# Moving two adaLN steps behind the norm's transposes at the change of layers, in a two-layer hybrid transformer step

## The chip, the core and the metric

One Trainium2 chip, one of its cores. TensorE (PE) multiplies, VectorE (DVE) and ScalarE (ACT) do elementwise work, GpSimd (POOL) some adds and small DMAs, and SyncE's queue (SP) issues the large weight loads. The metric is the device time of one execution in microseconds (us), as the median of several runs.

## The reference, cut to what matters

Two token groups of 128 tokens (a context group, g = 0, and a latent group, g = 1) go through the same two layers. All data are float32.

```python
def layer(x, cond, l, p, ctx):
    mod = jnp.einsum('...d,de->...e', jax.nn.silu(cond), p['w_ada'][l]) + p['b_ada'][l]
    sh1, sc1, g1, sh2, sc2, g2 = jnp.split(mod.reshape(-1, 1, 6 * D_MODEL), 6, axis=-1)
    hn = rmsnorm(x, p['norm_mix'][l]) * (1.0 + sc1) + sh1
    mix, ctx_tensors = token_mixers(hn, l, p, ctx)      # attention, retention, HGRN2; w_in, w_out
    x = x + g1 * mix
    hn = rmsnorm(x, p['norm_ffn'][l]) * (1.0 + sc2) + sh2
    x = x + g2 * moe(hn, l, p)                          # 16 experts, top 2 of the best group
    return x, ctx_tensors
```

D_MODEL is 1024; `w_ada` (1024 x 6144 a layer) makes the modulation, which people call adaLN; `w_in` is 1024 x 3840, and an expert has three matrices of 1024 x 512.

## The kernel before

Each engine has its own program, and semaphores order them. A `Ledger` counts what every semaphore has been raised to, so a wait names a label, such as `("xn1", 0, 1)`, and gets the right count. Both groups live in SBUF as rows, `x[:, g, :]`, and as features, `hnT`, eight chunks of 128 features by 256 tokens.

**Loads.** SP issues the weight loads of 1 MB each into `ring`, eight slots in turn, and into a few other tiles (`eP`, `wT` and the `home_` tiles), in one order fixed by hand. Before each load it waits until PE has released the slot. PE releases a slot with a later matmul: the slot's name is put on the list `owed`, and the next matmul that is given to `pay` raises the semaphore. An instruction of this kernel carries one increment, so a matmul that signals something else doesn't pay.

**adaLN steps.** The modulation of two of the six vectors, for both groups, is one accumulation over eight steps. `ada_step(l, what, k)` waits for one slot of `w_ada` and runs four matmuls of 512 columns, each with 32 columns of `silT` as its stationary side, into the four 32-partition strips of bank 1. The steps are spread over the kernel to keep PE busy while other engines work. Five of them, `IN_CHANGE`, which are the steps k = 0 to 4 of `(1, "g")`, stand at the change from layer 0 to layer 1. SP issues their loads behind the two loads of the first block of `w_in` ("f", into `eP` and `wT`).

**End of a layer.** The experts run in eight turns (a loop whose body is one round of all eight). In the last turn, and after it, `gates_to_all(g)` copies the gate row g2 of a group to all 128 partitions: for each half of 512 columns one matmul with 32 rows, from rows 64 to 95 of `modG` into bank 0 and from rows 96 to 127 into bank 1; ACT takes both halves into `gbuf2[g]`, which are the tiles `sq` and `t1`. Then four matmuls add the last turn's rows to banks 4 to 7 (group 0 halves 0 and 1, group 1 halves 0 and 1). DVE multiplies each bank by its gate half. The first half of a group goes to `first_product[g]` and POOL adds it to `x` (line 2019); the second goes to `nsq` and DVE adds it (line 1675).

**Start of layer 1.** ACT sums the squares of each group's row and makes 1/rms into `stat` (lines 1725, 1697, 1692). `normed("xn1", g)` on DVE scales the row in two halves into `xs` (line 1159). PE's `normalized_group` transposes the halves (four 128 x 128 blocks each), and `shifted` on DVE, or on ACT for the last half of group 1, applies scale and shift on the way into `hnT` (lines 1186 and 1762). The projection block "f" follows: `by_head_and_group` takes group 0 first, then transposes group 1 and takes that; then come `by_head("f", 1)`, "q", "a" and the first matmuls of HGRN2, `diagonal`, which wait for DVE's `gates` and `queries`.

Line 479 of the profile is `mm`, line 514 the transposes of `bank_of_transposes`, line 546 those of `normalized_group`, line 1673 DVE's product with the gate.

Of the kernel before, what the change touches and what calls it, by code (L numbers as in the profile page):

```python
# [15 lines left out]
P = 128  # L16
D = 1024
KC = D // P
L = 2
NG = 2  # L20
# [25 lines left out]
AT_CHANGE = 5  # L46
# [161 lines left out]
def build(nc, io, known, final=False):  # L208
# [3 lines left out]
    led = Ledger(known)  # L212
# [3 lines left out]
    with ExitStack() as ctx:  # L216
        sems = {}

        def S(name):
            if name not in sems:  # L220
                sems[name] = ctx.enter_context(nc.semaphore(name))
            return sems[name]
# [4 lines left out]
        ps = ctx.enter_context(nc.psum_tensor("ps", [P, 8, BLK], f32))  # L227
# [7 lines left out]
        modX, modG = sb("modX", BLK), sb("modG", BLK)  # L235
        modTs = sb("modT", L, 4, KC, NG)
        C = {}
# [123 lines left out]
        IN_CHANGE = [(1, "g", k) for k in range(AT_CHANGE)]  # L361
# [111 lines left out]
        def _(pe):  # L473
# [4 lines left out]
            def mm(*a, **k):  # L478
                ins = nc.tensor.matmul(*a, **k)  # L479
                return ins  # L480

            def pay(ins):

                if owed:
                    s = owed.pop(0)
                    ins.then_inc(S(f"{s}_spent" if s in KEPT else f"slot{s}_used"), 1)
                return ins
# [49 lines left out]
            def normalized_group(stage, factors, g, ahead=None, first=None):  # L537

                xv = xs[:, g].rearrange("p (k q) -> p k q", k=KC)
                for h in range(2):  # L540
                    b = claim_for_norm() if h or first is None else first
                    if not h and ahead is not None:
                        ahead(b)
                    pe.wait_ge(c.of(factors, g, h), c.at(factors, g, h))
                    for k in range(KH):
                        last = nc.tensor.transpose(ps[:, b, k * P:(k + 1) * P], xv[:, KH * h + k, :], C["ident"][:])  # L546
                        if k < KH - 1:
                            pay(last)
                    last.then_inc(c.fills(b, stage + "T", g, h), 1)
# [32 lines left out]
            for l in range(L):  # L582
# [3 lines left out]
                def modulation_by_feature(l, norm, b=0):  # L586
# [6 lines left out]
                            pay(last)  # L593
                    last.then_inc(c.fills(b, "modT", l, norm), 1)

                def at_change(b):

                    for step in IN_CHANGE:
                        ada_step(*step)

                if l == 0:
                    b = claim_for_norm()
                    for step in EARLY[0:5]:
                        ada_step(*step)
                        stream_zeros(b, 3)
                    pe.wait_ge(c.of("begin_dma"), c.at("begin_dma"))
                    normalized_group("hn1", "xn1", 0, first=b)
                    normalized_group("hn1", "xn1", 1)
                    for step in EARLY[5:]:
                        ada_step(*step)  # L610
                    modulation_by_feature(0, 0)
                else:
                    normalized_group("hn1", "xn1", 0, at_change)

                def wait_for_input(g, half):
                    label = ("hn1S", g, half) if l else (f"hn1S{g}", half)
# [25 lines left out]
                def by_head_and_group(name, p, ss, b):  # L642

                    for g in range(NG):
                        if l and g:
                            normalized_group("hn1", "xn1", 1)
                        for hl in range(2):
                            h = 2 * p + hl
                            for k in range(KC):
                                if not hl and not k % KH:  # L650
                                    wait_for_input(g, k // KH)
                                for d in range(2):
                                    col = 64 * h + 256 * d
                                    last = mm(ps[64 * d:64 * d + 64, b, 256 * hl + P * g:256 * hl + P * (g + 1)], by_k(ss[k // KH], 512)[:, k % KH, col:col + 64], hnT[:, k, tok(g)], start=(k == 0), stop=(k == KC - 1), skip_group_check=True)
                                    if not (g and hl and k == KC - 1 and d):
                                        pay(last)
                    last.then_inc(c.fills(b, "projP", name, p), 1)
# [329 lines left out]
                with pe.Fori(c.cum[l], until) as r:  # L987
# [42 lines left out]
                    def gates_to_all(g):  # L1030

                        for h in range(2):
                            pe.wait_ge(S(f"bank{h}_free"), c.claim(h))
                        for h in range(2):
                            strip = slice(32 * (2 + h), 32 * (2 + h) + 32)
                            row = 32 * (2 + h) + g
                            mm(ps[:, h, :], C["ident"][strip, row:row + 1].broadcast_to([32, P]), modG[strip, :], start=True, stop=True).then_inc(c.fills(h, "gate2P", g, h), 1)

                    pe.wait_ge(c.of("bias"), c.at("bias"))
                    gather()  # L1040
# [63 lines left out]
                    for g in range(NG):  # L1104
                        for h in range(2):
                            pe.wait_ge(c.of("ys", h), c.at("ys", h))
                            last = mm(ps[:, 4 + 2 * g + h, :], seatT[t % 3][:, g, :], ys[:, h, :], start=False, stop=True, skip_group_check=True)
                            if g or h:
                                last.then_inc(c.makes(f"round_sums{2 * g + h}", 0), 1)
                            else:  # L1110
                                pay(last)
                c.cum[l + 1] = count_of_rounds(pe, l + 1)
                led.where = f"A{l}"
                for b in range(4, 8):
# [5 lines left out]
        def _(dve):  # L1120
# [5 lines left out]
            def st(ins, *label):  # L1126

                ins.then_inc(c.makes(*(label or (step[0],))), 1)
                dve.wait_ge(S(c.last[0]), c.last_value())
# [21 lines left out]
            for l in range(L):  # L1151
# [3 lines left out]
                def normed(stage, g):  # L1155
                    dve.wait_ge(c.of(stage + "r", g), c.at(stage + "r", g))
                    for h in range(2):
                        half = slice(h * BLK, (h + 1) * BLK)
                        st(ts(xs[:, g, half], x[:, g, half], stat[:, g, 2:3], None, ALU.mult), stage, g, h)
# [12 lines left out]
                    st(stt(out=modTs[:, l, 2 * norm + 1], in0=modTs[:, l, 2 * norm + 1], scalar=1.0, in1=nrmTs[:, l, norm].rearrange("p (k o) -> p k o", o=1).broadcast_to([P, KC, NG]), op0=ALU.add, op1=ALU.mult), "modS", l, norm)  # L1172


                normed("xn1", 0)
                if not l:
                    normed("xn1", 1)
                def shifted(stage, a, halves):

# [485 lines left out]

                step[0] = "dve_step"
                led.where = f"A{l}"
                dve.wait_ge(S("gate2"), c.value("gate2", f"A{l}", 0))
                for g in range(NG):
                    for h, to in enumerate((first_product[g], nsq[:])):  # L1670
                        sums = f"round_sums{max(2 * g + h, 1)}"
                        dve.wait_ge(S(sums), c.value(sums, f"A{l}", 0))
                        tt(to, ps[:, 4 + 2 * g + h], gbuf2[g][:, h * BLK:(h + 1) * BLK], ALU.mult).then_inc(c.freed(("y", 2 * g + h), "x2p", g, h), 1)
                        dve.wait_ge(S(c.last[0]), c.last_value())
                    st(tt(x[:, g, BLK:D], x[:, g, BLK:D], nsq[:], ALU.add), "x2", g)


        @block.scalar
        def _(acte):
# [35 lines left out]
            for l in range(L):  # L1715
# [212 lines left out]
                with acte.Fori(c.cum[l], c.cum[l + 1]) as r:  # L1928
                    c.t = r
                    led.where = f"T{l}"  # L1930
                    step[0] = "act_turn"

                    def gathered(t):

                        led.turn = t
                        for half in range(2):
                            evac(("xT", half), None, "xTs", half, fn=lambda src: nc.scalar.copy(xT[:, KH * half:KH * (half + 1), :], src.rearrange("p (k s) -> p k s", k=KH)))  # L1937

                    gathered(0)
                    for t in range(TURNS):  # L1940
                        led.turn = t
                        acte.wait_ge(c.of("gu", 0), c.at("gu", 0))
                        st(ex_(ge, ps[:, 2], -1.0), "gexp")
                        evac(("actT",), None, "actTs", fn=lambda src: nc.scalar.copy(actT, src.rearrange("p (k s) -> p k s", k=KE)))  # L1944
                        if t + 1 < TURNS:
                            gathered(t + 1)
                            led.turn = t
                        else:
                            for h in range(2):
                                evac(("gate2P", 0, h), gbuf2[0][:, h * BLK:(h + 1) * BLK])  # L1950
                        evac(("yP", 0), ys[:, 0], "ys", 0)
                    for h in range(2):
                        evac(("gate2P", 1, h), gbuf2[1][:, h * BLK:(h + 1) * BLK])
                    acte.sem_inc(c.makes("gate2"), 1)
                step[0] = "act_step"
                led.where = f"A{l}"

# [195 lines left out]
```

## Time and profile before

| | us |
|---|---|
| median of 3 runs | 928.63 |
| lowest and highest of them | 927.77, 929.88 |
| the profiled execution's own time | 925.69 |
| its span, first to last instruction | 923.9 |

The profiled execution was somewhat faster than all three timed runs. PE is busy 875.4 us of the span (95%), its weight loads (PEld) 446.1 us, DVE 457.1 us (49%), ACT 165.3 us, POOL 79.5 us; the DMA engines moved 307.36 MB at a mean of 333 GB/s, and 420 GB/s where they are full. The first projection of layer 1 begins at about 484 us of the span. A matmul of 128 x 512 float32 is two records in the trace, and records of PE overlap, so the distance between starts tells more than a duration.

### The profile page before, as it was taken

How to read it: one execution, taken by the hardware profiler on the slowest of the kernel's cores; microseconds unless marked ns; L12 is line 12 of the kernel's file. 1: busy time of each engine (PE TensorE's matmuls, PEld its weight loads, DVE VectorE, ACT ScalarE, POOL GpSimd, SP SyncE). 2: the span in 40 equal slices, each digit the busy share in tenths (PEclk: the TensorE clock that was granted, in tenths of full speed). 3: DMA queues.
4: the chain of work that ended last, by engine and by line, in shares of the span. 5: the costliest groups of instructions: out<-in, count | busy, mean ns of one | idle time of the engine just before them, and what ended most of it. 6: DMA issues, size and time to landing. Idle time of an engine off the chain costs nothing.

```text
span 923.9 us, 13303 instructions
## 1 busy us (share of the span) xinstructions
PE 875.4 (95%) x4752; PEld 446.1 (48%) x4758; DVE 457.1 (49%) x839; ACT 165.3 (18%) x428; POOL 79.5 (9%) x110
## 2 busy tenths in 40 slices
PE   5899999999999999999989999999998999999997
PEld 1655565568733333333327455756874333333332
DVE  2485887653563332332236887876357322333222
ACT  2212015221211111110021301432220111111011
POOL 1112230000010000000011223000001000000001
PEclk9999999999999999999999999999999999999999
DMA  8997665868789999999996565474568999999992
GB/s 362 415 404 290 228 253 204 319 270 342 298 338 423 420 419 421 420 420 421 420 414 226 218 221 200 183 299 180 234 267 316 423 419 420 420 420 422 419 420 98
DMA packets 50316, 307.36 MB, mean 333 GB/s; under 512 B 8682, under 2 KB 8698, under 8 KB 16848
## 3 DMA queue, kind: packets, MB, share of 16 engines
q1 hardware_dynamic: 42368, 291.52, 78.1%
q0 software_dynamic: 4848, 12.40, 3.6%
q10 hardware_dynamic: 3040, 2.62, 0.8%
q8 instruction: 39, 0.64, 0.3%
q14 instruction: 21, 0.17, 0.0%
HBM read 305.46 MB, written 4.73 MB: 336 GB/s over the span
## 4 chain that ended last, share of the span: by engine, by line
PE 81%; DMA 7%; DVE 7%; issue 2%; ACT 1%; SPq 1%; DVEq 0%; ACTq 0%
PE ps L479 77%; PE ps L514 4%; DMA wT<-in_w_in 3%; DMA ring<-in_w_experts 3%; DMA ring<-in_w_ada 2%; DVE fa L1261 1%; DVE rt L1132 1%; PE ps L546 1%; SPq L392 0%; ACT eP L1692 0%; DVE xy L1267 0%; DVE proj L1595 0%; DVE hnT L1186 0%; DVE home_es L1278 0%; DVE proj L1305 0%
## 5 line engine op out<-in xcount | busy, mean ns | idle before, releaser
L479 PE MATMUL ps<-ring,proj 128*64 128x512 f32 x1024 | 283.2, 596 | 2.7 <-ACT proj L1944 1.7
L479 PE MATMUL ps<-ring,hnT 128*128 128x512 f32 (+1 forms) x576 | 204.4, 506 | 3.2 <-DVE hnT L1516 1.0
L479 PEld LDWEIGHTS ps<-ring,proj 128*64 128x64 f32 x1024 | 87.8, 137 | 138.7 <-issue 138.7
L479 PEld LDWEIGHTS ps<-ring,hnT 128*128 128x128 f32 x576 | 106.7, 191 | 77.6 <-issue 69.7
L1663 DVE COPY proj<-ps 128x512 f32<-128x512 f32 x16 | 11.1, 691 | 129.4 <-PE ps L479 129.4
L479 PE MATMUL ps<-home_ra,proj 128*64 128x512 f32 x128 | 57.6, 593 | 4.8 <-issue 4.8
L479 PE MATMUL ps<-ring,silT 128*32 128x512 f32 x384 | 47.6, 616 | 14.0 <-DMA ring<-in_w_ada 7.1
L479 PE MATMUL ps<-home_kd,proj 128*64 128x512 f32 x128 | 57.8, 594 | 0.0
L479 PE MATMUL ps<-home_qc,proj 128*64 128x512 f32 x128 | 57.6, 593 | 0.0
L1649 DVE RECIPROCAL proj<-proj 128x512 f32<-128x512 f32 x16 | 53.6, 3353 | 0.6
L1648 DVE TENSOR_SCALAR proj<-proj 128x512 f32<-128x512 f32 x16 | 6.8, 427 | 80.8 <-ACT proj L1692 80.8
L479 PE MATMUL ps<-hnT,ring 128*128 128x256 f32 x192 | 43.6, 382 | 0.0
L479 PE MATMUL ps<-proj,modX 128*128 128x512 f32 x80 | 38.7, 606 | 0.0
L479 PEld LDWEIGHTS ps<-hnT,ring 128*128 128x128 f32 x192 | 35.7, 190 | 5.9 <-issue 1.2
L479 PEld LDWEIGHTS ps<-home_ra,proj 128*64 128x64 f32 x128 | 17.1, 137 | 41.9 <-issue 41.8
L479 PEld LDWEIGHTS ps<-xy 64*128 64x128 f32 (+1 forms) x480 | 29.9, 188 | 12.0 <-issue 11.1
L1937 ACT COPY proj<-ps 128x512 f32<-128x512 f32 x32 | 18.7, 585 | 91.6 <-PE ps L514 75.0
L1944 ACT COPY proj<-ps 128x512 f32<-128x512 f32 x16 | 9.4, 585 | 143.6 <-PE ps L514 143.6
L479 PEld LDWEIGHTS ps<-home_qc,proj 128*64 128x64 f32 x128 | 17.4, 137 | 35.6 <-issue 35.3
L1692 ACT ACTIVATE proj<-ps 128x512 f32<-128x512 f32 x16 | 9.6, 597 | 128.2 <-PE ps L479 128.2
L479 PE MATMUL ps<-xy 64*128 64x64 f32 (+1 forms) x480 | 32.0, 275 | 0.1
L1692 ACT ACTIVATE eP<-ps,rt 128x128 f32<-128x128 f32 (+1 forms) x64 | 26.2, 417 | 23.2 <-DVE rt L1426 22.6
(271 smaller groups left out, 1054.0 us busy)
## 6 DMA issues: line engine op xcount, KB each, us to landing
ring<-in_w_experts SPq DMA_DIRECT2D x128, 1024.0 KB, 15.4
ring<-in_w_ada SPq DMA_DIRECT2D x48, 1024.0 KB, 9.8
ring<-in_w_in SPq DMA_DIRECT2D x24, 1024.0 KB, 8.5
home_qc<-in_w_experts SPq DMA_DIRECT2D x16, 1024.0 KB, 13.9
home_ra<-in_w_experts SPq DMA_DIRECT2D x16, 1024.0 KB, 18.0
home_kd<-in_w_experts SPq DMA_DIRECT2D x16, 1024.0 KB, 19.4
ring<-in_w_out SPq DMA_DIRECT2D x8, 1024.0 KB, 11.0
eP<-in_w_experts SPq DMA_DIRECT2D x4, 1024.0 KB, 10.4
```

What stands on the lines that cost most here:

```text
L479: ins = nc.tensor.matmul(*a, **k)
L514: last = nc.tensor.transpose(ps[:, b, i * P:(i + 1) * P], src, C["ident"][:])
L546: last = nc.tensor.transpose(ps[:, b, k * P:(k + 1) * P], xv[:, KH * h + k, :], C["ident"][:])
L1132: return v.tensor_reduce(out=out, in_=in_, axis=AX, op=op)
L1261: st(v.reciprocal(R, R))
L1648: st(ts(ge, ge, 1.0, None, ALU.add))
L1649: st(v.reciprocal(ge, ge))
L1663: v.tensor_copy(ys[:, 1], ps[:, 3]).then_inc(c.freed(("yP", 1), "ys", 1), 1)
L1692: return act_(out, in_, AF.Exp, scale=scale, **k)
L1937: evac(("xT", half), None, "xTs", half, fn=lambda src: nc.scalar.copy(xT[:, KH * half:KH * (half + 1), :], src.rearrange("p (k s) -> p k s ...
L1944: evac(("actT",), None, "actTs", fn=lambda src: nc.scalar.copy(actT, src.rearrange("p (k s) -> p k s", k=KE)))
```

## The change

1. `at_change` runs three of the five steps of `IN_CHANGE` ahead of group 0's transposes (`AT_CHANGE - NG` = 3). The fourth follows those transposes, the fifth the transposes of group 1.
2. `normed("xn1", 0)` of layer 1 moves on DVE: it stands between the two products of group 1 and the last addition, that of `x`'s second half of group 1.
3. Each of the banks 4 to 7 signals by its own matmul (`round_sums0` is new; the first matmul paid a slot before). DVE waits for its own bank, and for the gate of its own group (`gate2_0`, `gate2_1` for `gate2`).
4. `gates_to_all` splits each of its two matmuls of 512 columns into two of 256. The first part of each pays, since the first sum no longer does. All four calls of a kernel run (two groups, two layers) are split.

```diff
                 def at_change(b):
-                    for step in IN_CHANGE:
+                    for step in itertools.islice(in_change, AT_CHANGE - NG):
                         ada_step(*step)
...
                     normalized_group("hn1", "xn1", 0, at_change)
+                    ada_step(*next(in_change))
...
                         if l and g:
                             normalized_group("hn1", "xn1", 1)
+                            ada_step(*next(in_change))
...
-                            mm(ps[:, h, :], C["ident"][strip, row:row + 1].broadcast_to([32, P]), modG[strip, :], start=True, stop=True).then_inc(c.fills(h, "gate2P", g, h), 1)
+                            for part_ in range(2):
+                                sl = slice(256 * part_, 256 * (part_ + 1))
+                                last = mm(ps[:, h, sl], C["ident"][strip, row:row + 1].broadcast_to([32, P]), modG[strip, sl], start=True, stop=True)
+                                if not part_:
+                                    pay(last)
+                            last.then_inc(c.fills(h, "gate2P", g, h), 1)
...
-                            if g or h:
-                                last.then_inc(c.makes(f"round_sums{2 * g + h}", 0), 1)
-                            else:
-                                pay(last)
+                            last.then_inc(c.makes(f"round_sums{2 * g + h}", 0), 1)
...
-                normed("xn1", 0)
                 if not l:
+                    normed("xn1", 0)
                     normed("xn1", 1)
...
-                dve.wait_ge(S("gate2"), c.value("gate2", f"A{l}", 0))
                 for g in range(NG):
+                    dve.wait_ge(S(f"gate2_{g}"), c.value(f"gate2_{g}", f"A{l}", 0))
                     for h, to in enumerate((first_product[g], nsq[:])):
-                        sums = f"round_sums{max(2 * g + h, 1)}"
+                        sums = f"round_sums{2 * g + h}"
                         dve.wait_ge(S(sums), c.value(sums, f"A{l}", 0))
                         tt(to, ps[:, 4 + 2 * g + h], gbuf2[g][:, h * BLK:(h + 1) * BLK], ALU.mult)...
+                    if g and l + 1 < L:
+                        c.l, led.where = l + 1, f"L{l + 1}"
+                        normed("xn1", 0)
+                        c.l, led.where = l, f"A{l}"
                     st(tt(x[:, g, BLK:D], x[:, g, BLK:D], nsq[:], ALU.add), "x2", g)
...
                         evac(("yP", 0), ys[:, 0], "ys", 0)
+                    acte.sem_inc(c.makes("gate2_0"), 1)
                     for h in range(2):
                         evac(("gate2P", 1, h), gbuf2[1][:, h * BLK:(h + 1) * BLK])
-                    acte.sem_inc(c.makes("gate2"), 1)
+                    acte.sem_inc(c.makes("gate2_1"), 1)
```

## Rows read from the trace of the kernel before

**Rows 1.** The page's chain that ended last: shares of the span by engine

```profile
PE 81%; DMA 7%; DVE 7%; issue 2%; ACT 1%; SPq 1%; DVEq 0%; ACTq 0%
```

**Rows 2.** The chain in order of time, 460 to 520: start, duration, what

```profile
464.73 16.28 DMA ring<-in_w_ada
...
518.73 1.27 PE ps L479 x9
```

**Rows 3.** Timeline of PE: start, duration, operation, records, [idle before <-releaser]

```profile
469.28 1.13 PE L479 MATMUL ps<-modG,c_begin 32*128 32x512 f32 x4
470.33 3.70 PE L479 MATMUL ps<-proj 128*128 128x512 f32 x8
473.97 3.04 PE L479 MATMUL ps<-ring,silT 128*32 128x512 f32 x24
478.50 1.06 PE L479 MATMUL ps<-ring,silT 128*32 128x512 f32 x8 [1.49 <-DMA ring<-in_w_ada]
481.05 1.07 PE L479 MATMUL ps<-ring,silT 128*32 128x512 f32 x8 [1.49 <-DMA ring<-in_w_ada]
482.05 1.09 PE L546 MATMUL ps<-c_begin,xs 128*128 128x128 f32 x8
484.17 1.09 PE L479 MATMUL ps<-hnT,eP 128*64 128x128 f32 x16 [1.02 <-DVE hnT L1186]
...
488.44 1.09 PE L546 MATMUL ps<-c_begin,xs 128*128 128x128 f32 x8
490.65 1.09 PE L479 MATMUL ps<-hnT,eP 128*64 128x128 f32 x16 [1.12 <-DVE hnT L1186]
```

**Rows 4.** Timeline of PE's weight loads, the third adaLN step among them

```profile
475.94 0.16 PEld L479 LDWEIGHTS ps<-ring,silT 128*32 128x32 f32 x8 [0.96 <-DMA ring<-in_w_ada]
```

**Rows 5.** Timeline of DVE at the change of layers

```profile
472.43 0.69 DVE L1673 TENSOR_TENSOR proj<-ps,sq 128x512 f32<-128x512 f32 x1 [2.24 <-PE ps L479]
473.15 0.69 DVE L1673 TENSOR_TENSOR nsq<-ps,sq 128x512 f32<-128x512 f32 x1
473.88 1.14 DVE L1675 TENSOR_TENSOR x<-x,nsq 128x512 f32<-128x512 f32 x1
...
476.50 1.22 DVE L1675 TENSOR_TENSOR x<-x,nsq 128x512 f32<-128x512 f32 x1
477.75 1.01 DVE L1159 TENSOR_SCALAR xs<-x,stat 128x512 f32<-128x512 f32 x2
482.74 2.87 DVE L1186 TENSOR_SCALAR hnT<-ps,modT 128x128 f32<-128x128 f32 x8 [3.98 <-PE ps L546]
```

**Rows 6.** Timeline of ACT: group 0's sum of squares and 1/rms

```profile
475.05 1.06 ACT L1725 ACTIVATE sq<-x 128x1024 f32<-128x1024 f32 x1 [3.36 <-DVE x L1675]
...
476.56 0.20 ACT L1692 ACTIVATE stat<-stat 128x1 f32<-128x1 f32 x1
```

**Rows 7.** The first gates_to_all of layer 0, its records split by narrow windows

```profile
464.64 0.70 PE L479 MATMUL ps<-modG,c_begin 32*128 32x512 f32 x2
...
465.17 0.59 PE L479 MATMUL ps<-modG,c_begin 32*128 32x512 f32 x2
```

**Rows 8.** Stretches: busy time of each engine, PE's clock, DMA share, GB/s

```profile
495.00:519.00 24.00, 23.95 (x118) 14.69 (x113) 21.50 (x28) 1.85 (x3) 4.28 (x8) 1.00 0.41 142
519.00:700.00 181.00, 174.10 (x1051) 116.55 (x1052) 124.80 (x257) 47.81 (x150) 21.93 (x32) 0.99 0.60 231
706.00:900.00 194.00, 189.70 (x858) 69.45 (x854) 62.99 (x91) 21.17 (x36) 7.09 (x7) 1.00 1.01 418
620.00:625.00 5.00, 5.00 (x21) 2.19 (x21) 4.17 (x11) 0.97 (x3) 0.00 (x0) 0.72 1.01 421
```

**Rows 9.** What SP's queue waited for, 482 to 720: us in total, times, longest

```profile
SPq L392 <- PE ps L479: 110.2, 18, 26.2
```

**Rows 10.** Timeline of DVE at the end of the kernel

```profile
915.49 0.69 DVE L1673 TENSOR_TENSOR proj<-ps,sq 128x512 f32<-128x512 f32 x1 [2.25 <-PE ps L479]
...
919.56 1.20 DVE L1675 TENSOR_TENSOR x<-x,nsq 128x512 f32<-128x512 f32 x1
```

More of the change, by code:

```diff
@@ L594, in modulation_by_feature @@
                     last.then_inc(c.fills(b, "modT", l, norm), 1)
+                in_change = iter(IN_CHANGE)
                 def at_change(b):
-                    for step in IN_CHANGE:
+                    for step in itertools.islice(in_change, AT_CHANGE - NG):
                         ada_step(*step)
```

## The prediction

> **What bounds the kernel now.** I read the chain of waits first. PE holds 81% of it and DMA 7% [rows 1], so the time moves if PE's program moves, and only there. Around the changed code the chain leaves PE: from 464.73 it follows the loads of `w_ada` for 16.28 us [rows 2]. In PE's timeline three adaLN steps begin at 473.97, the fourth at 478.50 and the fifth at 481.05, each of the last two after an idle stretch that a `w_ada` load ended, and only at 482.05 do group 0's transposes start [rows 3]. Their input was ready long before: DVE had scaled the row by 477.75 + 1.01 = 478.76 [rows 5]. So here the layer waits for the loads of two steps whose result nobody needs yet.
>
> Then I asked who is behind. From 495 to 519 PE is busy 23.95 of 24.00 us, without slack [rows 8], while the chain goes through DVE's gates and comes back to PE at 518.73 [rows 2]. Both end together, and both begin with the projections of "f". What starts these earlier moves both alike.
>
> **Part 1, the two steps behind the transposes.** Nothing is removed, two steps move. I work out when the first projection, now at 484.17 [rows 3], could start. Three things come together there.
>
> PE: the third step starts at 475.94, when its load is there [rows 4]. It takes as long as the fifth, 482.05 - 481.05 = 1.0, so PE is ready to transpose at 476.95 and done 0.87 later. The fourth step's load is there at 478.50, and the step fills PE until 479.5. The fifth, whose load is there at 481.05, runs behind group 1's transposes: there PE needs 0.87 + 1.0 = 1.9 us in a stretch that lasts 490.65 - 488.44 = 2.21 now [rows 3]. Both steps are thus nearly free, because PE sits idle for 1.02 and 1.12 us there, waiting for DVE's shift [rows 3]. Without this cover each would cost its 1.0.
>
> DVE, with parts 2 and 3 in it: the second sum of group 0 comes as before, so DVE begins its second product at 472.43 and not at 473.15; that is one product, 0.72, earlier [rows 5]. The addition behind it then ends at 474.3. ACT needs 476.56 + 0.20 - 475.05 = 1.71 for 1/rms [rows 6], so it is there at 476.03; meanwhile DVE does group 1's two products, 1.44. The scaling takes 1.01, until 477.1. Now comes the addition that it was moved ahead of. It takes 1.22 at most, as in the row; without POOL adding beside it perhaps 0.69, as the product of the same size [rows 5]. DVE is free at 477.8 to 478.35. The shift of the first half takes 484.17 - 482.74 = 1.43 [rows 3, 5], so its result is there at 479.25 to 479.8.
>
> The later of 479.5 (PE) and 479.25 to 479.8 (DVE) gives 479.5 to 479.8; I take 479.7, as the longer addition is a measured row. That is **4.5 us earlier**. What is late next is DVE: it and the fourth step end within 0.3 us of each other. Group 1's factor is late by this order, since its addition ends at 478.35 and not at 477.72, but PE wants group 1 only after 488.44 - 484.17 = 4.3 us of group 0's work; DVE finishes scaling it at about 482.2, before 484.
>
> What the move does to SP: the issue order stays. The fifth step's slot is released about 4 us later, at 486, and the load that takes it, the first of block "b", is issued later. The DMA engines are at 0.41 of their time from 495 to 519 [rows 8], and "b" is used after 519, so this costs nothing. The bounds are 0 and the 2.5 us that one load takes (481.05 - 478.50, [rows 3]).
>
> **Part 2, the scaled row ahead of the addition.** It is in the sum above. Behind the addition the scaling would end at about 478.0 rather than 477.1, and the transposes of the second half later by as much, so it is worth at most 1.0 here. It costs ACT's second factor up to 0.6, which is covered.
>
> **Part 3, each bank signals.** At the end of the kernel the same 0.72 is gained: DVE's products and additions run without a gap from 915.49 to 919.56 + 1.20 [rows 10], and the output waits for the last. Here nothing can hide it: **-0.72**. The extra waits are for things long done: DVE's first product waits for both groups' gates now, and what released it at 472.43 was PE and not ACT [rows 5]. The released slot is 1, about 2 us earlier, for a load that queues behind full DMA engines: nothing.
>
> **Part 4, the split.** The four calls lie on PE's path: the last sums come right behind them, then the three steps, and in both layers DVE starts on those sums. One call takes 470.33 - 469.28 = 1.05 [rows 3]. The trace of before has no two matmuls in a row in the same strip of rows, so I must bound the cost s of a split. The four records of a call start two by two, at 464.64 and 465.17 [rows 7]: the two strips work side by side, each pair some 0.43 us apart, as eight records take 3.64 us [rows 3]. The parts now come in the order strip 2, strip 2, strip 3, strip 3, each half as long. If the strips still run side by side, s = 0. If only neighbours of different strips pair, the middle two do and there are three stretches of 0.43 in place of two: s = 0.43. If none pairs, four: s = 0.86. I take the middle: the rows show pairing between neighbours and nothing of an overtaking. One call's cost comes twice before the change of layers (2s) and twice before the end (2s), 1.7 us in all.
>
> The Trainium skill ("TensorE: Matmul & The Clock Gate", section "Part 3: Packing small matmuls — row/col tiling") says that matmuls start and end strictly in program order, and that only weight loads are pulled ahead. This speaks against the change, and by it the sum would be the one with s = 0.43. The starts of the rows are in order and fit it, but they would fit the other too.
>
> **The sum.** At the change of layers -4.5 + 0.86 = -3.6 (the third step is then ready 0.6 later too, but DVE decides). At the end -0.72 + 0.86 = +0.1. Total **-3.5 us**. Against the profile's own execution that is 925.69 to 922.2; against the median of the runs shown, 928.63 to 925.1. I predict by the median, 3 us above the profiled execution, and this distance is itself a warning about what one run tells.
>
> **Does the gain last?** From 519 to 700 the DMA engines are at 0.60, and SP waits for PE to release slots, 110.2 us in 18 waits [rows 8, 9]. All loads move with PE. From 706 to 900 they are full at 418 GB/s [rows 8], so that stretch is a length of DMA time, but its start is set by slots that PE releases, and so it moves as well.
>
> **The rivals.**
> - *The strips keep running side by side* (s = 0). All of the -4.5 and -0.72 stays: -5.2, 923.4. For it: pairs start within a rounding in [rows 7]. Against: the second strip's matmul would have to pass a waiting one. Chance 0.28.
> - *No pairing at all* (s = 0.86): -3.0 at the change, since 2s delays only DVE's path, +1.0 at the end: -1.9, 926.7. Chance 0.15.
> - *The gain is given back to the DMA engines*: if some load between 519 and 700 isn't late because of PE but because of the queue before it, the full stretch from 706 starts when it did. Then only the end counts: +0.1, 928.8. Against it: 0.60 in [rows 8]. Chance 0.08.
> - *The split costs more than it looks, and the kernel gets slower.* If a matmul of 256 columns in a strip that is still busy takes the whole latency of one by itself, 0.59 to 0.70 [rows 7], with two records in each of four parts, one call goes from 1.05 to 8 x 0.65 = 5.2, s = 4.1. The total is -5.2 + 4s, so it is slower from s = 1.3 on, and by this price it would be 12 us slower, 940. Against it: sixteen records of 128 columns take 1.09 in the row at 490.65 [rows 3], so a short record doesn't bear a fixed latency. Chance 0.04.
> - *The clock.* Between 620 and 625 the granted clock is 0.72 [rows 8]: for a part of it PE ran at the lower of its two levels, 1.2 GHz, though busy. This costs 5 x 0.28 = 1.4 us. A shift of all that precedes may lose this stretch or add another, so 1.4 either way on any case. As the outcome that decides, 0.03.
>
> The forecast itself has 0.42.
>
> **Range and chances.** Cases of one sign hold 0.85; within them 923.4 to 926.7. With 1.4 below for the clock, and above up to the near side of the given-back gain, 922.0 to 928.2 leaves out less than 0.2. A measurement of this kernel can tell about 0.2%, 1.9 us. Faster by more: the forecast, s = 0, and half of s = 0.86, 0.77. Within 0.2%: the other half, the given-back case, some of the clock's, 0.18. Slower 0.05.
>
> **What would show it.** PE's timeline after: three steps together, group 0's transposes near 477 to 478, a fourth step behind them, and the first projection at 480 to 480.6, its wait ended by DVE's shift. If it was ended by a `w_ada` load, part 1 fails. The records of `modG`: 8 in 1.05 us (s = 0), 1.5 (the forecast) or 1.9. DVE's two scalings of group 0 ahead of the addition. `diagonal`'s first matmul at about 515 and not 518.73; if it is there but the end isn't 3.5 earlier, the later stretches took it back, and the share of DMA and the clock of these stretches tell which. DVE's last product pair should start 0.72 closer to the first sum. The prediction is wrong mainly if the split costs otherwise than I take it, for it enters four times.

## The result, and the profile after

The changed kernel takes 919.59 us as the median of 4 runs (918.78 to 921.2); the kernel before took 928.83 us in its 4 runs, 9.2 us more. The ratio of the runs is 0.9923, with a 95% interval of 0.9897 to 0.9949. Two later sets, on two chips, gave 0.9929 (0.9909 to 0.9949) and 0.9934 (0.9908 to 0.9959). Few runs make an uncertain median here, so I go by all runs that have a granted clock on record: 926.9 us is the mean of 77 runs of the kernel before, 919.8 the mean of 16 of the changed one. By these the change makes the kernel 7.1 us faster, 0.77%. The prediction had 925.1 us, 3.5 us faster, and its range ended at 922.0. Direction and places were right, the size was half of what was measured.

The profiled execution of the changed kernel has a span of 918.3 us and a time of 920.11. Its PE timeline at the change of layers answers to [rows 3]:

```profile
470.71 1.14 PE L479 MATMUL ps<-modG,c_begin 32*128 32x256 f32 x8
471.78 3.70 PE L479 MATMUL ps<-proj 128*128 128x512 f32 x8
475.41 3.00 PE L479 MATMUL ps<-ring,silT 128*32 128x512 f32 x24
478.34 1.09 PE L546 MATMUL ps<-c_begin,xs 128*128 128x128 f32 x8
479.90 1.06 PE L479 MATMUL ps<-ring,silT 128*32 128x512 f32 x8 [0.47 <-DMA ring<-in_w_ada]
480.90 1.09 PE L479 MATMUL ps<-hnT,eP 128*64 128x128 f32 x16
...
485.11 1.10 PE L546 MATMUL ps<-c_begin,xs 128*128 128x128 f32 x8
486.14 1.06 PE L479 MATMUL ps<-ring,silT 128*32 128x512 f32 x8
487.33 1.09 PE L479 MATMUL ps<-hnT,eP 128*64 128x128 f32 x16
...
515.41 2.05 PE L479 MATMUL ps<-xy 128*128 128x128 f32 x16
```

The two executions are shifted against each other by 1.4 us that arose before this place, so distances are to be compared. From the start of the last gate call to the first projection of layer 1 it was 484.17 - 469.28 = 14.89 us [rows 3]; it is 480.90 - 470.71 = 10.19. The three steps now stand together, the transposes follow at once, and the fourth step fills the wait behind them. From the first projection to `diagonal` (xy) it is 34.5 us in both: what was gained is kept. The gate call has eight records for four, and takes 471.78 - 470.71 = 1.07 us where it took 1.05.

DVE's timeline answers to [rows 5, 10]:

```profile
473.01 0.69 DVE L1679 TENSOR_TENSOR proj<-ps,sq 128x512 f32<-128x512 f32 x1 [1.40 <-PE ps L479]
473.87 0.69 DVE L1679 TENSOR_TENSOR nsq<-ps,sq 128x512 f32<-128x512 f32 x1 [0.17 <-PE ps L479]
...
477.45 1.11 DVE L1165 TENSOR_SCALAR xs<-x,stat 128x512 f32<-128x512 f32 x2 [0.40 <-ACT stat L1702]
478.60 0.69 DVE L1685 TENSOR_TENSOR x<-x,nsq 128x512 f32<-128x512 f32 x1
479.42 2.86 DVE L1192 TENSOR_SCALAR hnT<-ps,modT 128x128 f32<-128x128 f32 x8
...
909.89 0.69 DVE L1679 TENSOR_TENSOR proj<-ps,sq 128x512 f32<-128x512 f32 x1 [1.40 <-PE ps L479]
910.75 0.69 DVE L1679 TENSOR_TENSOR nsq<-ps,sq 128x512 f32<-128x512 f32 x1 [0.17 <-PE ps L479]
911.48 1.01 DVE L1685 TENSOR_TENSOR x<-x,nsq 128x512 f32<-128x512 f32 x1
...
913.97 1.20 DVE L1685 TENSOR_TENSOR x<-x,nsq 128x512 f32<-128x512 f32 x1
```

The first product now waits 1.40 us for its own bank where it waited 2.24, and the second for its own, 0.17. The two scalings stand ahead of the addition, which takes 0.69 us when POOL has nothing beside it. The shift starts at 479.42 and its first half is done when the fourth step is: the two ends that the prediction had within 0.3 us of each other. At the end of the kernel, these are the last gate call before, with the second product and the first addition behind it, and the last gate call after:

```profile
912.34 1.13 PE L479 MATMUL ps<-modG,c_begin 32*128 32x512 f32 x4
916.22 0.69 DVE L1673 TENSOR_TENSOR nsq<-ps,sq 128x512 f32<-128x512 f32 x1
916.94 1.14 DVE L1675 TENSOR_TENSOR x<-x,nsq 128x512 f32<-128x512 f32 x1
...
907.59 1.14 PE L479 MATMUL ps<-modG,c_begin 32*128 32x256 f32 x8
```

After, DVE is done at 913.97 + 1.20, 7.58 us behind that start. Before, it ended at 920.76 [rows 10], 8.42 us behind.

The stretches answer to [rows 8]. The first columns are the stretch and its length, then PE, PEld, DVE, ACT and POOL busy, the granted clock of TensorE, the share of the DMA engines and GB/s:

```profile
519.00:700.00 181.00, 174.01 (x1057) 115.43 (x1057) 125.61 (x254) 48.04 (x149) 21.08 (x28) 1.00 0.62 235
706.00:900.00 194.00, 190.82 (x852) 70.29 (x850) 59.70 (x85) 21.18 (x36) 6.00 (x6) 0.99 1.01 416
```

The DMA engines are used as before, and the end of their full stretch comes earlier, as the share of their time from 900 to 904 shows, before (0.84) and after (0.02):

```profile
900.00:904.00 4.00, 4.00 (x14) 1.83 (x12) 0.69 (x1) 0.58 (x1) 0.00 (x0) 1.00 0.84 352
900.00:904.00 4.00, 4.00 (x23) 1.42 (x18) 0.00 (x0) 0.00 (x0) 0.00 (x0) 1.00 0.02 8
```

So nothing is given back to them, as one rival had it.

These are 4.70 + 0.84 = 5.5 us from the path. The runs show 7.1. The experiments are to say where the other 1.6 are, and which part of the change carries what.

### The profile page after: what moved, and what is told of

Its sections match the earlier page's. It is cut to its first block, busy times and chain, and to the rows that moved or that the text cites. A ratio compares the mean times of both kernels' runs of the same rounds, so it can differ in the third digit from the quotient of the medians.

```text
span 918.3 us, 13341 instructions
## 1 busy us (share of the span) xinstructions
PE 875.0 (95%) x4774; PEld 447.5 (49%) x4774; DVE 456.5 (50%) x839; ACT 165.5 (18%) x428; POOL 79.6 (9%) x110
## 4 chain that ended last, share of the span: by engine, by line
PE 81%; DVE 9%; DMA 5%; ACT 2%; issue 2%; SPq 1%; DVEq 0%; ACTq 0%
PE ps L479 77%; PE ps L514 4%; DMA wT<-in_w_in 3%; DMA ring<-in_w_experts 2%; ACT eP L1702 1%; DVE fa L1267 1%; DVE rt L1138 1%; DVE stat L1138 0%; SPq L392 0%; PE ps L546 0%; DVE proj L1601 0%; DVE eP L1448 0%; DVE xy L1273 0%; DVE x L1685 0%; DVE hnT L1192 0%
## 6 DMA issues: line engine op xcount, KB each, us to landing
eP<-in_w_experts SPq DMA_DIRECT2D x4, 1024.0 KB, 10.4
```

## The experiments

Eleven runs were made: the changed kernel twice more, the kernel before once more, and seven altered kernels, one of them twice. An altered kernel is the kernel before or the changed one with one thing altered, or two in the last. "Interval" below is the distance from the start of the last gate call of layer 0 to the first projection of layer 1, from the PE timeline: 14.89 before, 10.19 after.

**The changed kernel again, and the kernel before against itself.** No edit.

> The changed kernel, unaltered. Theory A (the change shortens the path by 4.7 us at the change of layers and 0.8 us at the end, and the rest of the 9.2 us between the medians is scatter of few runs): 5 to 6 us under the kernel before, and in the trace 470 to 484 shortened as in the first profile. Theory B (something else is gained as well, 3 to 4 us, that the one profile before did not show, since it was the fastest of its runs): 8 to 10 us.

> The kernel before, unaltered, timed against itself: it gives the scatter and a second profile. Theory A: no difference, and a span of 924 to 928 whose surplus over the first profile (923.9) lies in the first 100 us or in stretches at the lower clock, at other places than the change. Theory B: a surplus of some 3 us in one place that the changed kernel doesn't have, near the change of layers or in the expert turns.

Changed: 919.6 us in 6 runs, 0.9929 (0.9909 to 0.9949); the interval is 478.84 - 468.61 = 10.23. Before against itself: 927.09 in 12 runs, 1.0007 (0.9992 to 1.0022); 483.36 - 468.47 = 14.89. The path repeats to a few hundredths, while the times of the kernel before scatter from 922.5 to 929.9 over all sets. The scatter follows the clock: over the 77 runs of the kernel before, the time falls by 0.46 us for each 0.001 of the run's mean granted clock (correlation -0.76). And the clock isn't the same for both: the mean is 0.9897 for the kernel before (77 runs) and 0.9932 for the changed one (16 runs). The difference of 0.0035 is worth 3.5 x 0.46 = 1.6 us. Together with 5.5 this makes 7.1. So neither theory as written held. The rest goes with the clock, which differs by 0.0035 with a standard error of 0.0008, and not with one stretch that is always there.

**Part 1 alone.**

```diff
-                    for step in IN_CHANGE:
+                    for step in itertools.islice(in_change, AT_CHANGE - NG):
...
                     normalized_group("hn1", "xn1", 0, at_change)
+                    ada_step(*next(in_change))
...
                             normalized_group("hn1", "xn1", 1)
+                            ada_step(*next(in_change))
```

> Part 1 alone: two steps behind the transposes, DVE's order, the sums' signals and the gate matmuls as before. By the row of DVE the scaling of group 0 ends at 478.8, the shift of the first half 0.7 later than the transposes at best, so the first projection is at about 480.9 where before has 484.17: 3.2 to 3.5 us faster. If the rival is right that the steps are worth nothing without the other parts, under 1 us.

921.48 us in 6 runs, 0.9948 (0.9932 to 0.9965). PE's timeline:

```profile
472.13 1.13 PE L479 MATMUL ps<-modG,c_begin 32*128 32x512 f32 x4
473.19 3.70 PE L479 MATMUL ps<-proj 128*128 128x512 f32 x8
476.82 3.05 PE L479 MATMUL ps<-ring,silT 128*32 128x512 f32 x24
481.15 1.24 PE L546 MATMUL ps<-c_begin,xs 128*128 128x128 f32 x8 [1.28 <-DVE xs L1163]
482.32 1.06 PE L479 MATMUL ps<-ring,silT 128*32 128x512 f32 x8
483.32 1.09 PE L479 MATMUL ps<-hnT,eP 128*64 128x128 f32 x16
```

The interval is 11.19, so part 1 takes 3.7 us off the path by itself, a little more than expected. The times say 4.8 us (3.2 to 6.3), at a mean clock of 0.9923. What is left in it is seen at the transposes: PE waits 1.28 us for DVE's row. That is where parts 2 and 3 find their microsecond.

**All but part 1.**

```diff
-                    for step in itertools.islice(in_change, AT_CHANGE - NG):
+                    for step in in_change:
...
-                    ada_step(*next(in_change))
...
-                            ada_step(*next(in_change))
```

> All but part 1: five steps stay ahead of group 0's transposes. The loads of w_ada then still set the start of the transposes, so nothing is gained at the change of layers and 0.8 us at the end: 0.8 us faster than before. If DVE's earlier row or the split counts by itself, 2 us or more.

926.65 us in 12 runs, 1.0005 (0.9989 to 1.0021): no difference, where 0.8 us was expected, which lies inside the interval. So without part 1 the other three parts gain nothing at the change of layers. The end has its 0.84, and in the one profile the interval grew from 14.89 to 487.11 - 470.93 = 16.18. The timeline of PE and the stretches say why:

```profile
480.13 1.06 PE L479 MATMUL ps<-ring,silT 128*32 128x512 f32 x8 [1.50 <-DMA ring<-in_w_ada]
482.66 1.93 PE L479 MATMUL ps<-ring,silT 128*32 128x512 f32 x8 [1.47 <-DMA ring<-in_w_ada]
484.53 1.82 PE L546 MATMUL ps<-c_begin,xs 128*128 128x128 f32 x8
```

```profile
482.00:487.00 5.00, 3.69 (x16) 1.77 (x16) 1.31 (x4) 0.00 (x0) 0.00 (x0) 0.66 1.02 418
```

The fifth step and the transposes take nearly twice their time, as the granted clock is 0.66 in these 5 us: for much of them PE ran at 1.2 GHz. It stands behind two waits of 1.5 us. In the two profiles of the kernel before the clock is full at this place, but with the same waits this execution lost it. That led to the next kernel.

**The kernel before with the waits filled, twice.** Matmuls of zeros, which write to claimed banks that are overwritten later; no step moves.

```diff
                     for step in IN_CHANGE:
                         ada_step(*step)
+                        if step[2] in (2, 3):
+                            stream_zeros(b, 5)
...
-                if not l:
-                    stream_zeros(b, 5)
+                stream_zeros(b, 4 if l else 5)
```

> The kernel before, with TensorE kept busy in the waits of the change of layers: matmuls of zeros behind the third and the fourth adaLN step (5 each, about 1.1 us) and behind group 0's transposes (4). No step moves, so the path keeps its length. Theory A (the changed kernel beats its 5.5 us of path by 1.5 us because TensorE no longer idles there and is granted its full clock more often): the mean granted clock of the runs goes from 0.990 to 0.992 to 0.994, and the time is 0.5 to 1.5 us under the kernel before. Theory B (the surplus is chance): clock 0.990 and no difference, or some tenths slower.

> The kernel before with its waits at the change of layers filled by zeros, once more, since the first time the interval just touched no change. Theory A (less idling there keeps TensorE's full clock): mean clock of the runs about 0.993 against 0.990, time 1 to 2 us under the kernel before, the path from the last gate matmul to the first projection 14.9 us as before. Theory B (chance): clock and time as before.

First: 925.15 us, 0.9982 (0.9962 to 1.0001), mean clock 0.9931 over 12 runs. Second: 926.67, 0.9993 (0.9975 to 1.0012), mean clock 0.9913. The interval is 14.92 and 14.89, so the path is untouched. Neither set is clear by itself. The 24 runs together have a mean of 925.8 and a clock of 0.9922, against 926.9 and 0.9897: 1.1 us faster, with a standard error of 0.4, and the clock is worth 2.5 x 0.46 = 1.15. This speaks for theory A, less strongly than a clear interval would. Busy time of PE from 474 to 491, in the kernel before, the first filled one and the changed one:

```profile
474.00:491.00 17.00, 11.41 (x127) 6.37 (x128) 9.66 (x20) 4.73 (x12) 1.74 (x2) 1.00 1.02 413
```
```profile
474.00:491.00 17.00, 14.45 (x149) 8.03 (x144) 8.88 (x20) 4.81 (x12) 1.28 (x1) 1.00 1.02 412
```
```profile
474.00:491.00 17.00, 16.04 (x190) 10.11 (x190) 9.78 (x21) 4.80 (x12) 2.33 (x2) 1.00 1.03 412
```

**The two steps behind block f.** From the changed kernel, the two `ada_step` calls behind the transposes are taken out, and follow `by_head`:

```diff
                 by_head("f", 1, ss)
+                for step in (in_change if l else ()):
+                    ada_step(*step)
```

> The changed kernel with the fourth and fifth step taken out of the waits and put behind the block f, where TensorE has no slack. If the two waits hide the steps (1.0 us each): the first projection of layer 1 starts when it does in the changed kernel or a few tenths before it, the queries' matmul (xy) 2.0 us later against it, so 2 us slower than the changed kernel and 5 us faster than before. If the steps cost their time in the waits too, it is as fast as the changed kernel.

921.18 us in 8 runs (mean 922.1), 0.9933 (0.9911 to 0.9956).

```profile
480.21 1.09 PE L546 MATMUL ps<-c_begin,xs 128*128 128x128 f32 x8
482.71 1.09 PE L479 MATMUL ps<-hnT,eP 128*64 128x128 f32 x16 [1.41 <-DVE hnT L1192]
...
490.87 1.09 PE L479 MATMUL ps<-hnT,eP 128*64 128x128 f32 x16 [1.13 <-DVE hnT L1192]
```

The interval is 482.71 - 472.57 = 10.14, as in the changed kernel; the waits of 1.41 and 1.13 us are empty again. From the first projection to xy it is 520.59 - 482.71 = 37.88 and not 34.5. Of these 3.4 us, 1.7 are the clock, 0.79 of full over 8 us in this execution, and 1.7 are the two steps. The runs are 1.6 (medians) to 2.3 us (means, standard error 0.9) slower than the changed kernel's in other sets; the two ratios to the kernel before, 0.9933 and 0.9929, don't tell them apart. So it is the path that shows the cover to be worth nearly what the steps take; the times agree once the clock is taken out of them (below). Like the profile without part 1, this one lost the clock at the change, again with waits left empty there.

**Part 2 undone.** `normed("xn1", 0)` of layer 1 goes back behind the last addition.

> The changed kernel with part 2 undone: DVE scales group 0's row behind the last addition, as before. By the rows of the steps alone (3.7 us gained of 14.89) and of the changed kernel (4.7): the signals give 0.8 and the order what is left, so the first projection is 10.4 to 11.0 us behind the gates, and the time within 0.8 us of the changed kernel. If the order on DVE carries the gain with the steps, 2 us or more slower than it.

919.12 us in 6 runs, 0.9911 (0.9882 to 0.9939), no slower than the changed kernel. The interval is 482.72 - 472.38 = 10.34, just under the 10.4 to 11.0 expected, so the order on DVE is worth 0.1 to 0.15 us. The transposes wait 0.47 us for DVE, and then the fourth step, whose load had come meanwhile, ends as late as the shift.

**Gate matmuls in eight parts.**

```diff
-                            for part_ in range(2):
-                                sl = slice(256 * part_, 256 * (part_ + 1))
+                            for part_ in range(8):
+                                sl = slice(64 * part_, 64 * (part_ + 1))
```

> The changed kernel with each gate matmul in eight parts of 64 columns, all eight of one strip of rows ahead of the eight of the other. If the second strip's matmuls run beside waiting ones of the first (s = 0, as two parts suggest), a call takes 1.1 us still, or a few tenths more for 32 records; if only close neighbours pair, 1.6 to 1.9 us.

```profile
464.43 3.39 PE L479 MATMUL ps<-modG,c_begin 32*128 32x64 f32 x32
467.75 3.65 PE L479 MATMUL ps<-ring,proj 128*64 128x512 f32 x16
```

One call takes 3.32 us; both expectations missed. The one run took 930.06, where four calls at 2.25 more each, against the changed kernel, would give 928.6. Why it takes so long is seen when the records of this call start, and when ACT finds the banks full (a bank is filled by one strip):

```profile
464.43:465.82 1.39, 1.39 (x13) 1.00 0.97 398
466.52 0.58 ACT L1714 COPY sq<-ps 128x512 f32<-128x512 f32 x1 [6.64 <-PE ps L479]
467.91 0.58 ACT L1714 COPY sq<-ps 128x512 f32<-128x512 f32 x1 [0.81 <-PE ps L479]
```

The first line is a stretch with PE's busy time and records, its clock, the DMA share and GB/s. In its 1.39 us 13 records start, one after the other, all of the first strip: the second start comes after 0.16 us, each further one after 0.112. Only then does the second strip begin, beside the last three of the first. ACT takes the first bank 2.09 us after the start and the second 1.39 us after that. So with eight parts the strips run mostly one after the other. With two parts they are a pair from the first record to the last (its first and last records in narrow windows), and ACT takes both banks without a pause, 1.21 us after the start of the first call at 466.06:

```profile
470.71 0.49 PE L479 MATMUL ps<-modG,c_begin 32*128 32x256 f32 x2
471.46 0.39 PE L479 MATMUL ps<-modG,c_begin 32*128 32x256 f32 x2
467.27 1.20 ACT L1714 COPY sq<-ps 128x512 f32<-128x512 f32 x2 [5.77 <-PE ps L479]
```

In both kernels the second strip begins when three records of the first are still to come: of 16, and of four. And within one strip a record of 64 columns follows another after 0.112 us, where those of 256 columns start at 471.03, 471.24 and 471.46, 0.216 us apart; at their rate it would be 0.216 / 4 = 0.054.

**The shift ahead of the addition.** A try at a faster version, and the changed kernel beside it:

```diff
-                    shifted("hn1", 0, ((0, 0), (0, 1)))
+                    shifted("hn1", 0, ((0, 0),))
+                    st(tt(x[:, 1, BLK:D], x[:, 1, BLK:D], nsq[:], ALU.add), "x2", 1)
+                    shifted("hn1", 0, ((0, 1),))
```

with the load of `wT` behind that of the fourth step.

> The changed kernel again, beside the next one on the same chip. Theory A: 5.5 us of path and 1.5 us of clock, together 7 us under the kernel before (0.9925), mean clock of the runs about 0.994.

> The changed kernel with DVE's shift of group 0's first half ahead of the last addition of x, and the load of wT behind that of the fourth adaLN step. In the changed kernel the first projection waits for that shift (479.42 + 1.43) and for the fourth step, whose load comes at 479.90. With both earlier it should start 0.4 us sooner, 9.8 us behind the gates where the changed kernel has 10.2. If the addition that is now late delays group 1's factor more than its 2 us of slack, the projection of group 1 is late by what is missing and the gain is gone.

Changed kernel: 919.62 us, 0.9934 (0.9908 to 0.9959), mean clock 0.9920 in these 6 runs. The other: 919.71 in 12 runs, 0.9937 (0.9916 to 0.9958).

```profile
477.85 1.09 PE L481 MATMUL ps<-hnT,eP 128*64 128x128 f32 x16
480.05 1.09 PE L481 MATMUL ps<-hnT,wT 128*64 128x128 f32 x16 [1.11 <-DVE hnT L1194]
```

The first projection starts 9.55 us behind the gates, 0.6 earlier. But the second half of the shift comes behind the addition, PE waits 1.11 us for it where it waited 0.35, and the gain is given back within 3 us: the second projection starts 11.75 us behind the gates, where the changed kernel has 482.34 - 470.71 = 11.63. DVE's work until the second half is the bound in both orders. The start was expected at 9.8 us. The gain was expected to go, if it went, by group 1's factor; it went by the second half of group 0's own shift.

**All runs at equal clock.** One fit to the 161 runs of eight kernels, with one slope for the clock (it comes out as 0.50 us for each 0.001) and one offset for each kernel, takes the clock out of the times (it doesn't tell the chips apart). The offsets against the kernel before can be laid beside the gain that the profiles show on the path, at the change and at the end:

| kernel | runs, mean clock | gain on the path | gain in time at equal clock |
|---|---|---|---|
| before | 77, 0.9897 | | |
| changed | 16, 0.9932 | 5.5 | 5.4, standard error 0.4 |
| part 1 alone | 6, 0.9923 | 3.7 | 4.0, 0.5 |
| all but part 1 | 12, 0.9895 | 0.8 | 0.4, 0.4 |
| steps behind block f | 8, 0.9920 | 5.5 - 1.7 = 3.8 | 3.7, 0.5 |
| part 2 undone | 6, 0.9943 | 5.4 | 4.9, 0.6 |
| shift ahead of the addition | 12, 0.9935 | 5.5 | 4.7, 0.4 |
| before, waits filled | 24, 0.9922 | 0.0 | -0.1, 0.3 |

Path and time agree within two standard errors in every row. And the mean clock is higher in each kernel that has the two steps moved or the waits filled, but not in the one that has every part but the first.

## Why the prediction was wrong

**The way and the place: right.** The wait for the loads of two steps that nobody needs yet was the bound, PE and DVE share the start at "f", and the whole shift reached the end. Most of its named signs are there: the three steps together, the full DMA stretch moved along, xy earlier (515.41 in an execution that ran 1.4 us late, so 4.7 us earlier than before). One is there only in part: the first projection was to wait for DVE's shift, and it follows the fourth step without a wait, 0.1 us behind the end of the shift's first half; that step itself had waited 0.47 us for its load. The wait for the shift, 0.35 us, is at the next projection.

**Part 1 to 3 at the change: right, a little short.** The term was -4.5, measured 4.70. Inside it, part 1 alone gives 3.7 and the rest 1.0; of this the signals give nearly all. The bound of at most 1.0 for part 2 was kept, at 0.1 to 0.15.

**Part 3 at the end: right.** -0.72, measured 0.84. DVE's second product begins 0.72 earlier behind the gate call, as forecast, and the addition beside POOL took 1.01 rather than 1.14 us.

**Part 4, the first step that failed.** "I take the middle": s = 0.43, four times, 1.7 us. Measured is 1.07 - 1.05 = 0.02. The forecast needed the second strip's parts to wait behind the first strip's, which would have taken 1.5 us. One record of 256 columns lasts half of the 0.43 us of one of 512; eight one after another would take 1.7. They took 1.07 with the gap, and their records start in pairs from the first to the last, so two ran side by side throughout, although the code gives both parts of one strip ahead of the other. The prediction saw "nothing of an overtaking" in its rows, which had only one waiting record to overtake; here the second strip goes ahead of three. The rule of the Trainium skill that the prediction weighed ("TensorE: Matmul & The Clock Gate", section "Part 3: Packing small matmuls — row/col tiling") would have given 1.5, if the order of the code were that of the engine; this trace doesn't agree with that reading. Whether the order was changed on the way from the code to the engine or by the engine, no run here shows. The eight parts show that the free split has an end, and for two reasons: the second strip went ahead of three records and not of more, so the strips ran mostly one after the other, and a record of 64 columns took twice its share of the time. Four parts were not run. Two slips of the prediction's sums change nothing: the rival that gets slower adds 4 x 4.1 - 5.2 = 11.2 us and not 12, and -3.0 + 1.0 is -2.0 and not -1.9.

**The clock, the second step that failed.** It stood in the prediction as 1.4 us either way by luck, with no mean. It has one. The changed kernel has PE busy 16.0 of 17 us where it was busy 11.4, and its runs are granted 0.0035 more of the clock, 1.6 us. The filled kernel, which has only this, recovers about 1.1 us. That the clock can be lost at the change is shown by two profiles, both with waits left empty there (0.66 from 482 to 487 and 0.79 from 482 to 490). That the idling explains the whole 1.6 us is supported by means over runs, and not settled. The profiles of the kernel before itself keep the full clock at the change, and most profiles lose it at other places too: 0.87 over 612 to 625 in both of the kernel before and in none of the changed one, but also in two kernels that have the steps moved (steps behind block f, part 2 undone). How less idling at the change would spare the clock elsewhere, no run shows.

**The level.** 928.63, the median of 3 runs, is 1.7 us above the mean of 77. A forecast of a time inherits this error; the prediction noted the 3 us to the profiled execution and took the median all the same.

The miss of 5.5 us is thus 1.7 for the split, 0.3 for the two small terms, 1.6 for the clock and 1.7 for the level, 5.3 in sum. The case s = 0 in the range gave 5.2 us for the path, and the path measured 5.5.

## What to carry to other kernels

Where an engine waits for data of work that nobody needs yet, put that work behind the next thing that is needed, into a wait that is at least as long; here two steps of 1.0 us sat in waits of 1.4 and 1.1 us for nothing. Such a move can gain twice, once on the path and once in the granted clock, as the means over runs suggest here; compare path lengths in the trace for the first and the mean granted clock over many runs for the second. Where times scatter by the clock, fit the clock out of them before laying them beside the path. Splitting small matmuls in two strips in two parts was free here, in eight parts it was not.

## What the runs showed of the hardware

- Matmuls in two different strips of 32 rows ran side by side although the code gives two matmuls of one strip ahead of two of the other: 8 records of 256 columns in 1.07 us. With eight matmuls of each, the second strip began only when 13 of the first strip's 16 records had started, so it went ahead of three waiting records in both kernels.
- Float32 records of 32 rows that follow each other in one strip start 0.216 us apart at 256 columns and 0.112 us apart at 64.
- An addition of 128 x 512 float32 on DVE, both sides in SBUF, took 0.69 us alone and 1.00 to 1.22 us with POOL adding beside it.
- The time of one and the same kernel scatters over 922.5 to 929.9 us with the granted clock, 0.46 us for each 0.001 (0.50 in the fit over eight kernels), while its path between two matmuls repeats to some hundredths.
